# Heads taken in pairs, values computed token by token, linears moved to the end of a branch, last picks singly

## The reference, cut to what matters

```
x = x + 0.5 * swiglu(rms_norm(x), w13, w2)
h = rms_norm(x);  aq, ak, av, bq, bk, bv, cq, ckv, ckr = split(h @ w_in)
oa = diff_attention(...)   # a: 4 heads, each two score maps of width 64; all keys; p1 - lam*p2
ob = window_gqa(...)       # b: 8 heads of width 64, 2 key heads, window of 3 blocks, sinks
oc = mla(...)              # c: 4 heads, score = 128 wide part + 64 wide rope part; values from ckv @ w_ukv
x = x + (sum over a, b, c of sigmoid(h @ w_gate + b) * (o @ w_branch)) @ w_out
x = x + 0.5 * swiglu(rms_norm(x), w13, w2)
```

## Time and profile before

| | |
|---|---|
| median of 3 runs | 4615.15 us (4614.6 to 4616.44) |
| the profiled execution's own time | 4613.27 us |
| span of the profiled execution | 4611.5 us, granted TensorE clock 0.968 on average |
| TensorE matmul busy | 4237.9 us (92%), 15888 instructions |
| VectorE busy | 2554.1 us (55%) |
| ScalarE busy | 1336.9 us (29%) |
| GpSimd busy | 1956.9 us (42%) |
| HBM | 174 GB/s over the span; about 420 GB/s in the PEER stage |

### The profile page before, as it was taken

The page is one execution under the profiler, slowest core; times in us unless marked ns, Lnnn a source line. Parts: engine busy times, 40 slices in busy tenths (PEclk is TensorE's granted clock), DMA queues, the critical chain, the costliest instruction groups (busy, mean ns, idle before and its releaser), DMA issues.

```text
span 4611.5 us, 49856 instructions
## 1 busy us (share of the span) xinstructions
PE 4237.9 (92%) x15888; PEld 2847.3 (62%) x15888; DVE 2554.1 (55%) x4576; ACT 1336.9 (29%) x2902; POOL 1956.9 (42%) x1614
## 2 busy tenths in 40 slices
PE   7999987787878787899999999999999999999998
PEld 4467753333333333488866666888888857767887
DVE  7967776766767675544244634542343265536442
ACT  2224222222222222332223333322322133323222
POOL 4333543333333333344454353544444534345443
PEclk8999999989998999999999999999999999999999
DMA  5122279999999999632321121223223312112332
GB/s 138 41 64 69 74 294 422 421 422 421 421 411 420 413 421 419 249 100 93 94 78 64 38 83 60 96 96 94 97 97 94 95 43 71 57 60 86 100 97 81
DMA packets 161750, 806.09 MB, mean 175 GB/s; under 512 B 17616, under 2 KB 26240, under 8 KB 96000
## 3 DMA queue, kind: packets, MB, share of 16 engines
q0 software_dynamic: 73728, 536.90, 28.1%
q1 hardware_dynamic: 83104, 260.15, 17.5%
q10 hardware_dynamic: 4704, 6.42, 0.8%
HBM read 798.17 MB, written 5.24 MB: 174 GB/s over the span
## 4 chain that ended last, share of the span: by engine, by line
issue 28%; PE 26%; POOL 19%; DMA 15%; DVE 9%; ACT 2%; POOLq 1%; DVEq 1%; ACTq 0%
POOL wl L590 10%; PE bank L950 7%; DMA rows_o<-in_peer_uv,expert 6%; POOL wl L559 5%; PE bank L643 5%; PE bank L645 5%; PE bank L644 5%; DMA rows_x<-in_peer_uv,expert 5%; DMA rows_w<-in_peer_uv,expert 4%; POOL wh L557 2%; DVE rows_x L2001 1%; DVE hst L1779 1%; DVE rows_o L2001 1%; DVE rows_w L2001 1%; POOLq L558 1%
## 5 line engine op out<-in xcount | busy, mean ns | idle before, releaser
L590 POOL TENSOR_TENSOR wl<-raw,wh 128x1024 fp32r<-128x1024 f32 (+3 forms) x314 | 735.0, 2342 | 823.3 <-ACT wh L1423 823.2
L643 PE MATMUL bank<-xh,wh 128*128 128x512 f32 x2496 | 997.2, 400 | 4.4 <-DVE xl L1541 2.2
L645 PE MATMUL bank<-xh,wl 128*128 128x512 f32 x2496 | 975.5, 391 | 0.0
L644 PE MATMUL bank<-xl,wh 128*128 128x512 f32 x2496 | 974.1, 390 | 0.0
L643 PEld LDWEIGHTS bank<-xh,wh 128*128 128x128 f32 x2496 | 469.7, 188 | 166.5 <-issue 72.1
L1423 ACT ACTIVATE wh<-raw 128x1024 fp32r<-128x1024 f32 x314 | 331.2, 1056 | 718.3 <-PE bank L645 550.0
L645 PEld LDWEIGHTS bank<-xh,wl 128*128 128x128 f32 x2496 | 469.7, 188 | 99.6
L644 PEld LDWEIGHTS bank<-xl,wh 128*128 128x128 f32 x2496 | 470.5, 189 | 94.3 <-issue 2.4
L559 POOL TENSOR_TENSOR wl<-raw,wh 128x1024 fp32r<-128x1024 f32 (+2 forms) x232 | 474.7, 2046 | 34.6 <-issue 1.9
L950 PE MATMUL bank<-rows_o,diag 128*128 128x512 f32 x688 | 338.6, 650 | 90.2 <-ACT diag L1389 90.1
L950 PE MATMUL bank<-rows_x,diag 128*128 128x512 f32 x688 | 338.8, 650 | 87.4 <-ACT diag L1389 87.4
(11 more groups left out here) (378 smaller groups left out, 6593.6 us busy)
## 6 DMA issues: line engine op xcount, KB each, us to landing
raw<-in_w_l SPq DMA_DIRECT2D x320, 512.0 KB, 3.3
raw<-in_w SPq DMA_DIRECT2D x58, 512.0 KB, 3.3
raw<-in_w_l SPq DMA_DIRECT2D x64, 448.0 KB, 3.3
raw<-in_w_l SPq DMA_DIRECT2D x56, 256.0 KB, 2.6
raw<-in_w SPq DMA_DIRECT2D x16, 256.0 KB, 2.6
bias_scratch<-brow ACTq DMA_DIRECT2D x1, 3072.0 KB, 33.2
raw<-in_uq_l SPq DMA_DIRECT2D x16, 192.0 KB, 2.3
rows_o<-in_peer_uv,expert POOLq DMA_INDIRECT x172
```

The source lines that it names most:

```text
L590: gp.tensor_tensor(wl[:, slot, 0:w], raw[:, rslot, 0:w], f32(wh[:, slot, 0:w]), ALU.subtract).then_inc(w_split.sem, 1)
L643: pe.matmul(bank[b][:], wh[:, slot, c], ah, start=k == 0, stop=False)
L644: pe.matmul(bank[b][:], wh[:, slot, c], al, start=False, stop=False)
L645: mm = pe.matmul(bank[b][:], wl[:, slot, c], ah, start=False, stop=k == last)
```

## The change

1. Mixer attention, b and c: items are ordered in pairs of heads (2h, 2h+1), block by block. At each even step TensorE issues the score matmuls of both items of the pair, one head on partitions 0 to 63 and one on 64 to 127, into `score[0]` and `score[1]`; it waits first until both banks have been read. In c the two 128 row parts come first, then the two rope parts. `pt` gets a second buffer in c (`oraw`), and each head is summed when its fourth block is turned, two heads after steps 8 and 16.
2. Values of a and c are computed with the activations as the stationary operand and the weights as the moving one, so that they come out with tokens on partitions. The transposes and `vf` go. In a each token's scale is needed as a column: four extra matmuls with one column each and an Ln and an Exp on ACT. ACT reads the values straight out of the banks into `vt`.
3. The weights of c's values become two tiles of 128x512; the first two chunks of `out` are whole tiles.
4. `in_b0` gets the fourth query chunk of b (`in_b` loses it). Chunk 0 runs whole in step 16 of a, the first half of chunk 1 in step 17, its second half ahead of the sums of squares.
5. Mixer attention: DVE splits `total` into high and low when it reads it; the eight splits after the loop go.
6. The last four picks of PEER are handled one by one instead of as a group of four.

```diff
-    "in_a": whole(12, 8), "gate_a": whole(8, 8), "in_b0": whole(3, 8), "br_a": whole(8, 4),
-    "in_b": whole(4, 8), "gate_b": whole(8, 8), "br_b": whole(8, 4),
-    "in_c": whole(7, 8), "uq": whole(8, 3), "ukv": whole(8, 2), "gate_c": whole(8, 8), "br_c": whole(8, 4),
-    "out": [[(0, 4), (4, 8)]] * 2 + whole(6, 8), "up2": FFN_UP, "down2": FFN_DOWN,
+    "in_a": whole(12, 8), "gate_a": whole(8, 8), "in_b0": whole(4, 8), "br_a": whole(8, 4),
+    "in_b": whole(3, 8), "gate_b": whole(8, 8), "br_b": whole(8, 4),
+    "in_c": whole(7, 8), "uq": whole(8, 3), "ukv": whole(4, 2), "uv": [[(0, 4)], [(0, 4)], [], []], "gate_c": whole(8, 8), "br_c": whole(8, 4),
+    "out": whole(8, 8), "up2": FFN_UP, "down2": FFN_DOWN,
...
+            def value_linear(at_, j0, l, operand):
+                part = at_.chunks[j0:j0 + NB]
...
+                    pe.wait_ge(w_split.sem, w_split.at(tile + 1, l))
+                    for m in range(per_tile):
+                        k = n * per_tile + m
+                        ah, al = operand(k)
+                        c = slice(m * T, (m + 1) * T)
+                        for tb in range(NB):
+                            b, k_use = chunk_bank(at_, j0 + tb)
+                            if k == 0:
+                                pe.wait_ge(acc_read[b].sem, acc_read[b].at(k_use, l))
+                            r = slice(tb * P, (tb + 1) * P)
+                            pe.matmul(bank[b][:], ah[:, r], wh[:, slot, c], start=k == 0, stop=False)
+                            pe.matmul(bank[b][:], al[:, r], wh[:, slot, c], start=False, stop=False)
+                            mm = pe.matmul(bank[b][:], ah[:, r], wl[:, slot, c], start=False, stop=k == last)
+                    mm.then_inc(product.sem, 1)
+            def token_sum(l):
+                wait_turn(l)
+                for tb in range(NB):
+                    mm = pe.matmul(turn[:, tb:tb + 1], square_sum[:, tb * P:(tb + 1) * P], ones[:, 0:1], start=True, stop=True)
+                mm.then_inc(turned.sem, 1)
...
@@ mixer attention, TensorE
-                if j < pairs:
-                    h, g = divmod(j, 2)
-                    r = 64 * (h % 2)
+                if j < pairs and j % 2 == 0:
                     if j >= 2:
-                        pe.wait_ge(score_read.sem, score_read.at(s0 + j - 1, None))
+                        pe.wait_ge(score_read.sem, score_read.at(s0 + j, None))
+                    h, g = item_1(j)
                     for n in range(2):
...
+                        for m in range(2):
+                            r = 64 * m
+                            mm = pe.matmul(score[m][:, (2 * n + 2 - nk) * P:(2 * n + 2) * P], q1[r:r + 64, h // 2, qb * P:(qb + 1) * P],
+                                           q1[r:r + 64, 8 + h // 4, k0:k0 + nk * P], start=True, stop=True)
...
-                linear(AT_1["br_a"], j, None, normed, ready)
+                linear(AT_1["br_a"], j, None, lambda k: (q1h[:, k, :], attended_low(k)), (total_read, t0))
@@ a, TensorE
                 sum_squares(l)
-                for j in range(2, 12):
+                token_sum(l)
+                for j in range(2, 8):
                     linear(AT_L["in_a"], j, l, normed)
-                values(4, l, lambda f: vf[:, f, :], AT_L["in_a"], 8)
+                value_linear(AT_L["in_a"], 8, l, normed)
...
+                    elif s == 16:
+                        linear(AT_L["in_b0"], 0, l, normed)
+                    else:
+                        linear(AT_L["in_b0"], 1, l, normed, share=(0, 2))
...
-                linear(AT_L["in_b0"], 0, l, normed, share=(0, 2))
+                linear(AT_L["in_b0"], 1, l, normed, share=(1, 2))
                 batch(BATCH_A, BANKS_A, l)
-                linear(AT_L["in_b0"], 0, l, normed, share=(1, 2))
-                for j in range(1, 3):
+                for j in range(2, 4):
                     linear(AT_L["in_b0"], j, l, normed)
@@ b, TensorE
-                    if s < items_b:
+                    if s < items_b and s % 2 == 0:
+                        if s > 1:
+                            pe.wait_ge(score_read.sem, score_read.at(32 + s, l))
+                        h, qb = item_b(s)
...
+                        for m in range(2):
+                            r = 64 * m
+                            pe.matmul(score[m][:, 0:(hi_ - lo_) * P], qk[r:r + 64, h // 2, qb * P:(qb + 1) * P],
+                                      qk[r:r + 64, 4 + h // 4, lo_ * P:hi_ * P], start=True, stop=True).then_inc(scored.sem, 1)
@@ c, TensorE
-                            pe.wait_ge(exp_ready.sem, exp_ready.at(48 + s - 1, l))
+                            pe.wait_ge(exp_ready.sem, exp_ready.at(48 + s, l))
+                        for m in range(2):
+                            pe.matmul(score[m][:], qk[:, h + m, qb * P:(qb + 1) * P], qk[:, 6 + h + m, :], start=True, stop=False)
+                        for m in range(2):
+                            r = 64 * m
+                            pe.matmul(score[m][:], qk[r:r + 64, 4 + h // 2, qb * P:(qb + 1) * P], qk[r:r + 64, 10, :],
+                                      start=False, stop=True).then_inc(scored.sem, 1)
@@ ACT
+            def token_root(l):
+                act.wait_ge(turned.sem, turned.at(use.next("turn"), l))
+                inverse_root(v_scale, turn[:, 0:NB], D).then_inc(turn_read.sem, 1)
+                act.drain()
...
+                    act.activation(vt[:, tb, :], bank[b][:], ACT.Copy, scale=v_scale[:, tb:tb + 1] if scaled else 1.0).then_inc(acc_read[b].sem, 1)
...
+                sizes = [QUAD] * (WINDOW // QUAD) if q < WINDOWS - 1 else [QUAD] * (WINDOW // QUAD - 1) + [1] * QUAD
@@ DVE, mixer attention
-                    dve.tensor_copy(q1[:, (j - 7) // 4, :], total[:]).then_inc(total_read.sem, 1)
+                    split(total[:], q1h[:, (j - 7) // 4, :], attended_low((j - 7) // 4)).then_inc(total_read.sem, 1)
...
-            for j in range(8):
-                split(q1[:, j, :], xh[:, j, :], xl[:, j, :]).then_inc(op_ready.sem, 1)
```

165 lines of the change are left out of this document (93 added, 72 removed).

## The result

| | before | after |
|---|---|---|
| median on the same chip | 4615.22 us (4614.6 to 4616.44) | 4572.91 us (4571.47 to 4577.98) |
| span of the profiled execution | 4611.5 us | 4572.1 us |

A forecast was written before the change was run, and what follows sets the result against it. TensorE was taken to bound the attention loops and stretches between them, until DVE becomes slower. Savings of 16.8 + 20 + 11 + 4.4 + 4.3 + 8 + 16.4 + 12.6 - 2 = 91.5 us gave 4524 us, range 4508 to 4558.

The forecast's parts named there:

- Pairs and values in c: c, both layers: paired rope scores save 16.8 us; values with fewer waits and no transposes save 12.6.
- End of a: End of a: 36 matmuls of later linears fill TensorE's wait for probabilities, saving 16.4 us in both layers.
- Values in a: a: the four transposes before the first score go, four one-column matmuls come in; 8 us saved in both layers.
- The readout split behind the mixer attention: After the mixer attention loop: `br_a`'s first chunk no longer waits for a split at each k; 4.4 us saved.
- Last picks: End of PEER: single picks are ready earlier than a group of four, so TensorE ends sooner; 4.3 us saved.
- they are level, so neither hides the other's bursts; I take 11: Mixer attention loop: TensorE needs 112.7 us, DVE 113.2; of 15.3 us of saved score slots, 11 were counted.
- the new wait ends earlier than one that stands right behind it, and is priced at nothing: Paired scores: waiting until both score banks are read costs nothing; b was to gain 10 us a layer.
- Its load can only start when the first tile's rest is formed, now 1.2 us later: Start of `out`, third whole tile's load: last operand has 0.85 us of cover; 1 us a layer charged.
- Just in time: Feed forward after PEER: could begin at 1922.3 instead of 1926.71, with POOL's second tile done at 1922.33.
- rival 1: Pairs do not overlap in their new places; 47.8 us of the sum go, kernel 4571; chance 0.06.
- Rival 2: DVE becomes the bound in b and mixer attention, so 31 us stay in the loops, kernel 4555; chance 0.10.
- Rival 3: Slower: TensorE and DVE stand for each other at 64 pairs; at 2 us idle per pair, 4652; chance 0.03.

The follow-up runs named there:

- best kernel: Kernel after, plus POOL held back and scaling ahead of the read in even steps in mixer attention and b, `out` in half tiles: 4529.77 us, ratio 0.9811.

## Why the prediction missed

**Right, with their sizes.** Pairs and values in c: 30.4 measured, 29.4 forecast (6.0 a layer and one more is 13.0, where the sum took 12.6). A tile's time was not the same "whatever its width", though: before, from issue to landing it took 1.9 us for 128 KB and 3.2 for 512 KB. End of a: 15.8 against 16.4; the 3.75 us wait is gone, and the head's values run at full clock (compare):

```profile
2449.13 0.65 PE L756 MATMUL bank<-ident,work 128*128 128x128 f32 x4
...
2455.09 0.60 PE L756 MATMUL bank<-ident,work 128*128 128x128 f32 x4
...
2458.31 3.60 PE L1060 MATMUL bank<-pt,vt 128*128 128x512 f32 x8
```

Values in a: 7.2 against 8. The added root on ACT took 3.1 us, forecast 3.2, and stayed covered; the Exp begins 0.01 us behind its load here too (the rows are rounded), so the drain that the Trainium skill (ScalarE: Activation LUTs, What ACT_TABLE_LOAD costs) adds to each load is again not seen:

```profile
2312.86 1.28 ACT L1186 ACT_TABLE_LOAD   x1
2314.16 0.20 ACT L1186 ACTIVATE stat<-stat 128x4 f32<-128x4 f32 x1
```

The readout split behind the mixer attention: 4.5 against 4.4. Last picks: 3.5 at their place against 4.3. The wait for both score banks was also priced rightly: TensorE stands for it once in the mixer attention, 1.0 us, and never in b.

**Wrong in the mixer attention (18.4 us).** The step was "they are level, so neither hides the other's bursts; I take 11". I counted a burst as a DVE instruction that "lasts twice as long" beside POOL, so as a share of DVE's load. The runs show a hold until POOL's instruction ends, whatever the held one's own size, and paid in full, and with a fallen clock on top, when TensorE's next transposes need it. POOL's start hangs on TensorE's end of a gate chunk, DVE's order on the items, so every edit to either moves the meeting by some tenths of a microsecond, and each period repeats it. The same work came out at 149.4 or 131.4 us (singles), at 141.0 or 124.3 (pairs) by that place. The forecast priced what each engine has to do, and never asked where POOL's instruction falls in DVE's new order. With that mended, pairs against single items are 7.6 us (131.4 to 123.8), of 11. The best kernel's loop is 8.6 us below the kernel before, but POOL's place and DVE's order were improved in it too, and never in a kernel with single items and a plain readout.

**Wrong in b (15.3 us).** The step was "the new wait ends earlier than one that stands right behind it, and is priced at nothing". The new wait did cost nothing; the one behind it, for the scaling, had cost 0.5 us in b and now costs 8.5 a layer, and that was taken as unchanged. The order it argues from is the fault: the scaling of the odd item before stands *behind* the read of the next pair's first score, so DVE idles in front of a score with ready work queued behind it. With single items TensorE did a score between the one that DVE waited for and the transposes that need the scaling; with pairs the even step's score is directly followed by them, one score less of distance. What the runs show is that turning these two gives 5.9 us a layer with POOL held back, and POOL's place 2.5, and that DVE's waits for scores and TensorE's for the scaling both shrink with it; that the lost distance is what made them is this argument, not a measurement. The rest was sound: with both mended b is 94.5 where 95.3 was forecast. The rows of the stall in b:

```profile
2555.35 2.35 POOL L583 TENSOR_TENSOR wl<-raw,wh 128x1024 fp32r<-128x1024 f32 x1
...
2555.60 2.31 DVE L1714 TENSOR_SCALAR work<-work,stat 128x384 f32<-128x384 f32 x1
...
2558.04 0.44 PE L756 MATMUL bank<-ident,work 128*128 128x128 f32 x2 [2.81 <-DVE work L1714]
```

**Wrong at `out` (12.0 us).** "Its load can only start when the first tile's rest is formed, now 1.2 us later" looked at the tiles' arrival. The tiles were in time; their subtractions are twice as long, follow each other without a pause and hold the last `mixl`. The cover of 0.85 us was right and was the warning: it is less than one such hold (2.2 us for `mixl_last`).

**Wrong behind the picks (5.1 us).** "Just in time" was asked of POOL's second tile. What was late is DVE's chain behind it, which meets the subtractions of the third and fourth tiles. The gain of 3.5 was given back there in full.

**The rivals.** The result, 4573, lies 2 us from rival 1's 4571, and rival 1 is wrong in every row that bears on it: a total names no cause, and that agreement is chance. Rival 2 (DVE the bound) is wrong as well, since the loops fell to 120.0 and 94.5 with DVE's instructions as they were; its rows, TensorE waiting for DVE's probabilities, were seen, but for another reason. The rule that the prediction quoted from the Trainium skill (TensorEngine Tiling (Array Packing), PSUM Bottleneck) does not explain it: DVE's reads of scores keep their 477 ns in the mixer attention. Rival 3 had a part of it, each side standing for the other: TensorE's waits for the scaling are 20.9 us over the 16 pairs of the mixer attention and 8.5 over b's 16 in layer 0, but c's 16 pairs have none. DVE's waits for scores in b, forecast to fall from 19 to about 9, fell to 16.4. The best kernel, 4529.8, is 6 us from the forecast's 4523.7: the gains were there, and 43 us of them were lost in meetings of POOL and DVE and in one order.

## What to carry to other kernels

When a change moves the rhythm of a loop, list the long instructions of POOL with what starts them, lay them over DVE's new order, and charge the full hold where one meets a scaling, or an instruction with two inputs in SBUF, that somebody waits for. If it is bad, move POOL by one wait: that is cheap, and here such waits in two loops gave 15.6 us together. Compare by stage, since two opposite effects of 10 us can leave the total where it was.

## What the runs showed of the hardware

- POOL's subtraction of a tile (2.34 to 2.44 us in the loops, two inputs in SBUF) holds some DVE instructions that work between SBUF and SBUF until it ends: the scaling (0.35 to 2.04), and those with two inputs in SBUF, additions and subtractions of 512 columns (0.68 to 2.85) and even a minimum on two columns (0.16 to 2.33). Its cast of 1.04 us holds the scaling (0.29 to 0.84) and the minimum (0.16 to 1.02) too. DVE instructions with an input in PSUM (0.35 and 0.48) and reductions from SBUF (0.69) kept their durations beside it in every kernel, for instance in the timeline of the last kernel above. So did a reciprocal of two values in SBUF, 0.17 us at 433.76 in the kernel after, 0.22 behind the start of the subtraction that then held the scaling. Which of the two is held goes by who starts first: `mixl_last`, 0.06 ahead of POOL's subtraction, kept its 0.68, and POOL's took 1.77 where 1.29 is usual. The Trainium skill (SBUF — State Buffer, Who interferes with whom) has this as a rule: the two engines share a pair of ports, taken as a lock for a whole instruction, by a `tensor_scalar` in its two-port mode or an instruction with two inputs in SBUF, and never by a reduction on trn2; whoever comes second "fully blocks". All rows here agree, and a forecast made with it would have looked for the meetings.
- TensorE's clock falls after such a stand and takes the next matmuls with it: behind waits of 2.42 and 2.28 us the granted clock is 0.50, the level of 1.2 GHz, and matmuls of 512 columns have 0.63 where 0.39 is usual. In the mixer attention the granted clock was 0.97 before, 0.94 after and 0.99 in the best kernel. So a hold costs more than its length: with POOL held back, 7.5 us less were held up and the loop was 12.2 shorter.
